# A decoder trunk on one core: the second mixer's work laid out in a table of slots, its time step on 128 columns, and a look-ahead in the residual step

## What is computed

```python
for i in range(4):
    x = x + mixer[i](rmsnorm(x, mix_norm[i]))
    x = x + conv_ffn(rmsnorm(x, ffn_norm[i]), ...)      # D_FF 2816
```

```python
z, xbc, dt_raw = split(h @ w_in)                 # 2048, 3072, 32 columns
xs, B, C = split(silu(causal_conv4(xbc)))
dt = softplus(dt_raw + dt_bias)                  # (512, 32)
cs = cumsum(dt * a) in each chunk                # a = -exp(a_log)
y = (C B^T * exp(cs_l - cs_s), causal) @ (x * dt)  +  C @ state * exp(cs)  +  x * d_skip
y = group_rmsnorm(y * silu(z)) * norm_w;  out = y @ w_out
```

## Time and profile before

| | |
|---|---|
| median of 3 runs | 2025.08 us (2021.57 to 2025.17) |
| the profiled execution | 2023.04 us, span 2021.2 us |
| busy in the span: PE, DVE, ACT, POOL | 91%, 60%, 56%, 58% |
| granted TensorE clock, mean of the execution | 0.972 of full |
| DMA, mean | 111 GB/s |

### The profile page before, as it was taken

One profiled execution on the slowest core, in us unless ns is written; L12 is line 12 of the kernel. 1 busy time (PEld: TensorE's weight loads), 2 busy tenths in 40 slices (PEclk: granted clock), 3 DMA queues, 4 the chain that ended last, 5 costly groups with the idle time before them and its releaser, 6 DMA issues.

```text
span 2021.2 us, 25413 instructions
## 1 busy us (share of the span) xinstructions
PE 1845.0 (91%) x8918; PEld 1152.6 (57%) x8918; DVE 1213.3 (60%) x1995; ACT 1132.2 (56%) x1571; POOL 1171.9 (58%) x1678
## 2 busy tenths in 40 slices
PE   6978999978888888999999778899999999879999
PEld 3544666644554554566665566466666777546665
DVE  6774777146667654577414665577526777467740
ACT  6867666436655635666545444666553444566642
POOL 4536778845334334777785201677785555367786
PEclk9999999999999989999999888999999999989999
DMA  5314444433122222444443100344443222134443
GB/s 195 104 42 146 146 146 148 155 102 105 58 68 71 66 63 84 166 147 146 145 158 105 42 1 22 116 147 149 142 157 108 84 84 84 63 115 148 148 151 127
DMA packets 64926, 225.00 MB, mean 111 GB/s; under 512 B 7328, under 2 KB 8736, under 8 KB 64544
## 3 DMA queue, kind: packets, MB, share of 16 engines
q1 hardware_dynamic: 64224, 221.69, 32.4%
q10 hardware_dynamic: 576, 1.69, 0.3%
HBM read 221.25 MB, written 2.10 MB: 110 GB/s over the span
## 4 chain that ended last, share of the span: by engine, by line
PE 66%; DVE 15%; ACT 13%; issue 5%; DMA 1%; POOL 0%; DVEq 0%; ACTq 0%; SPq 0%
PE psum L274 20%; PE psum L284 19%; PE psum L316 10%; PE psum L320 9%; PE psum L1521 3%; ACT w_big L232 2%; DVE psum L1316 1%; ACT arena L1982 1%; ACT x_big L352 1%; DVE arena L2072 1%; DVE arena L2077 1%; ACT psum L1195 1%; ACT psum L356 1%; DVE x_resid L422 1%; DVE psum L1409 1%
## 5 line engine op out<-in xcount | busy, mean ns | idle before, releaser
L248 POOL TENSOR_TENSOR w_rest<-w_panel,w_big 128x256 bf16<-128x256 f32 (+1 forms) x1674 | 1171.7, 740 | 836.5 <-ACT w_big L232 836.2
L274 PE MATMUL psum<-x_big,w_big 128*128 128x512 f32 x2248 | 667.6, 429 | 53.2 <-ACT x_big L352 37.4
L284 PE MATMUL psum<-x_rest,w_rest 128*128 128x512 bf16 x2248 | 561.2, 385 | 0.2 <-DVE x_rest L388 0.2
L232 ACT ACTIVATE w_big<-w_panel 128x1024 fp32r<-128x1024 f32 (+3 forms) x425 | 422.8, 1018 | 240.0 <-DVE x_resid L422 115.5
L274 PEld LDWEIGHTS psum<-x_big,w_big 128*128 128x128 f32 x2248 | 419.6, 190 | 186.4 <-issue 44.2
L284 PEld LDWEIGHTS psum<-x_rest,w_rest 128*128 128x128 bf16 x2248 | 190.2, 99 | 283.2 <-issue 108.0
L574 DVE SCALAR_TENSOR_TENSOR psum<-ffn_raw,params,psum 128x512 f32<-128x512 f32 x352 | 264.5, 751 | 6.2
L566 DVE TENSOR_TENSOR ffn_raw<-psum,rstd 128x512 f32<-128x512 f32 x176 | 121.7, 692 | 153.2 <-PE psum L284 132.7
L316 PE MATMUL psum<-g_big,w_big 128*128 128x512 f32 x704 | 199.3, 423 | 0.0
L528 ACT ACTIVATE psum<-ffn_raw,params 128x512 f32<-128x512 f32 x176 | 137.7, 782 | 107.3 <-DVE ffn_raw L566 106.8
L422 DVE SCALAR_TENSOR_TENSOR x_resid<-psum,x_resid 128x512 f32<-128x512 f32 x64 | 43.9, 688 | 210.6 <-PE psum L320 210.6
(11 more groups left out here) (255 smaller groups left out, 1925.1 us busy)
## 6 DMA issues: line engine op xcount, KB each, us to landing
w_panel<-in_up SPq DMA_DIRECT2D x176, 512.0 KB, 3.4
w_panel<-in_dn SPq DMA_DIRECT2D x64, 448.0 KB, 3.1
w_panel<-in_ssd_in SPq DMA_DIRECT2D x41, 512.0 KB, 3.5
w_panel<-in_dn SPq DMA_DIRECT2D x32, 512.0 KB, 3.4
w_panel<-in_hgrn_in SPq DMA_DIRECT2D x32, 512.0 KB, 3.5
w_panel<-in_lru_in SPq DMA_DIRECT2D x19, 512.0 KB, 3.4
w_panel<-in_ssd_out SPq DMA_DIRECT2D x16, 512.0 KB, 3.5
w_panel<-in_swa_in SPq DMA_DIRECT2D x12, 512.0 KB, 3.5
```

Of the source, the lines that this page charges most:

```text
L232: act.activation(k.w1[:, slot, lo:words], k.w[:, slot, lo:words], ACT.Copy, scale=(SHIFT - 1) / SHIFT).then_inc(k.s("panel_big"), 1)
L248: rest = pool.tensor_tensor(k.w2[:, slot, a], k.w[:, slot, a], k.w1[:, slot, a].bitcast(F32), ALU.subtract)
L274: pe.matmul(out, k.w1[:, slot, q * m:(q + 1) * m], k.x1[:, q, :], start=q == 0, stop=False)
L284: mm = pe.matmul(out, k.w2[:, slot, q * m:(q + 1) * m], k.x2[:, q, :], start=False, stop=q == DT - 1)
```

## The change

- **Slots.** `ssd_events()` now runs over slots n = 0 to 48. In slot n PE makes projection tile n (of 40, in three pieces of 2, 2 and 4 reduction steps), DVE scales tile n-1 (`evict`) and adds its taps, ACT adds its bias and applies silu. Group g's `turn` is in slot 10, 20, 30, 39, its states one slot later, its four pairs of heads in the four slots after that, its norm 7 slots after `turn`.
- **Gating in the next slot.** A pair's `seg`, `spread` and `out` stand in one slot; DVE's part after `out` (`post`) comes first in the next slot, then the two products of `seg`, and the three taps last. The sum of squares has an event of its own (`sum`). `finish` is cut into `normed` and `rest`, spread over two slots. The order of the tiles in a group changes (`SSD_KINDS`), and with it the order of the columns of the weight.
- **Time step on 128 columns.** The first tile holds the 32 columns four times. DVE moves chunk c (128 tokens) of copy c to partitions 32c to 32c+31, so that the chain runs on 128 partitions by 128 columns, in three pieces in slots 0 to 2; the scan needs no resets. ACT lays the three bf16 parts out again (12 copies of 32x128).
- **Selection columns.** The 128 equal columns that pick a head out of `cs3` are no longer copied out for each group (L1354, L1356): PE reads one column with a step of 0, and ACT copies out the 64-wide ones once (`pick64`).
- **Residual.** In `residual_vector`, after the output projections of mixers 1, 3 and 4, add(o) stands ahead of split(o-1) and squares(o-1). In all of them split of the last tile comes ahead of the last two sums, and ACT's last two squares and last panel come last. In the feed-forward net the norm's matmul stands after the high half of tile 1 (it stood after tile 0).

Core of the diff:

```diff
 def residual_vector(dve, k, c, job):
+    ahead = job in ("lru_out", "swa_out", "hgrn_out")
     for o in range(DT):
         add_to_residual(dve, k, job, o)
-        if c is not None:
+        if c is None:
+            continue
+        if o and ahead:
+            split_x(dve, k, c, o - 1)
+            if o < DT - 1:
+                sum_squares(dve, k, c, o - 1)
+        elif not ahead and o < DT - 1:
             split_x(dve, k, c, o)
-            sum_squares(dve, k, c, o)
+            if o < DT - 2:
+                sum_squares(dve, k, c, o)
+    if c is not None:
+        split_x(dve, k, c, DT - 1)
+        sum_squares(dve, k, c, DT - 2)
+        sum_squares(dve, k, c, DT - 1)
...
 def residual_scalar(act, k, c, job):
+    n = len(OUT_PARTS[job])
     for o in range(DT):
+        last = out_panel(job, o, n - 1)
+        if n > 1 or o == DT - 1:
+            round_ahead(act, k, job, last - 1 if n > 1 else last - 2)
+        act.wait_ge(k.s("banks_free"), k.evicted(job, o))
+        if o < DT - 2:
             round_ahead(act, k, job, last)
+        scaled_x(act, k, c, o)
+        if o < DT - 2:
+            square_x(act, k, c, o)
+    square_x(act, k, c, DT - 2)
+    square_x(act, k, c, DT - 1)
+    round_ahead(act, k, job, last)
...
 def ffn_tensor(pe, k, l):
         in_begin(pe, k, job, i)
-        in_tile(pe, k, job, i, fresh=None if i else 2 * l + 1)
-        if i == 0:
+        in_big(pe, k, job, i, fresh=None if i else 2 * l + 1)
+        if i == 1:
             norm_tensor(pe, k, 2 * l + 1)
+        pe.wait_ge(k.s("panel_split"), k.split(job, i))
+        in_rest(pe, k, job, i, fresh=None if i else 2 * l + 1)
...
+SSD_KINDS = [[6, 7, 0, 1, 2, 3, 4, 5, 8, 9]] + [[0, 1, 2, 3, 6, 4, 5, 7, 8, 9]] * (SSD_G - 1)
+SSD_LAST = 10 * SSD_G
+SSD_TURN = [10, 20, 30, 39]
...
+    head_at = {at + 2 + p: (g, p) for g, at in enumerate(SSD_TURN) for p in range(SSD_R // 2)}
+    norm_at = {at + 7: g for g, at in enumerate(SSD_TURN)}
...
+    for n in range(SSD_LAST + 9):
+        if n == SSD_LAST:
+            tiles = [[], fill(1), fill(1)]
+        elif SSD_LAST < n < SSD_LAST + 6:
+            tiles = [fill(1), [], fill(1 if n < SSD_LAST + 3 else 2)]
...
+        if n == SSD_LAST + 6:
+            ev += fill(16 - early)
...
+    def pick(self, g, r):
+        return self.pick3[0:SSD_ROWS, SSD_R * g + r:SSD_R * g + r + 1].to_broadcast([SSD_ROWS, P])
...
     def dt(g, i):
+        if i == 0:
+            dve.wait_ge(k.s("panel_used"), k.used(job, 0))
+            for c in range(NC):
+                rows, cols = slice(32 * c, 32 * c + 32), slice(c * P, (c + 1) * P)
+                dve.tensor_tensor(b.cs[rows], k.ps[rows, k.bank(job, 0), cols], k.rstd[rows, cols], ALU.mult
...
+            softplus_begin(dve, softplus, b.cs, b.size, b.dt)
+        elif i == 1:
+            softplus_ratio(dve, k, "ssd_softplus", softplus, b.size, b.e, b.q, b.e2)
+            softplus_series(dve, softplus, b.size, b.e2, (15, 13, 11, 9, 7, 5, 3))
```

More of the change, by code:

```diff
@@ L1001, in ssd_events @@
[L1001 to L1012 removed]
+    turn_at = {at: g for g, at in enumerate(SSD_TURN)}
@@ L1246, in early @@
             round_ahead(act, k, "ssd_out", len(used) - 1)
-    do = {"dt": dt, "conv": conv, "decays": decays, "turn": turn, "seg": seg, "out": out, "norm": norm,
-          "finish": finish, "early": early, "silu": silu, "spread": spread}
+    do = {"dt": dt, "cs": cs, "evict": evict, "decays": decays, "scores": scores, "seg": seg, "square": square, "root": root,
+          "normed": normed, "early": early, "silu": silu, "spread": spread, "round": round_}
     for what, g, i in ssd_events():
@@ L1426, in ssd_vector @@
+    do = {"dt": dt, "evict": evict, "taps": taps, "decays": decays, "table": table, "turn": turn, "states": states,
+          "seg": seg, "post": post, "sum": sum_, "normed": normed, "rest": rest}
     for what, g, i in ssd_events():
@@ L2302, in layout @@
         i[:, None] % SSD_DT == np.arange(SSD_DT),
[L2303 removed]
+        np.ones((P, P)),
     ], axis=1).astype(np.float32)
```

484 lines of the change are left out of this document (269 added, 215 removed).

## The result

The changed kernel takes **1924.3 us** (median of 4 runs, 1923.6 to 1925.8) against 2024.0 (4 runs, 2021.6 to 2025.2): ratio **0.951**, interval 0.949 to 0.953, 99.7 us less. The forecast was 1933 with a range of 1914 to 1964: the sign and the range hold, the size was 9 us too small. In the profiled executions the span went from 2021.2 to 1921.8, 99.4 less.

What follows compares the result with a forecast made beforehand. PE, at work nine tenths of the span, was taken as the bound. From 2023.0 us, 58.7 (second mixer) and 33.2 (look-ahead and last tile) go, leaving 1931.1; with 2.1 for the median, 1933 us, range 1914 to 1964.

Steps and rivals of the forecast that it cites:

- The large idle piece: Start of the second mixer: with the time step on 128 columns, PE's idle 15.7 us go.
- Waits inside the pairs: Second mixer's pairs of heads: PE's short waits go, with gating in the next slot; no separate size given.
- slots would be limited by DVE or ACT: Rival, second mixer: each of 16 slots with heads grows by 1.2 us; 25 us come back, 1958 us; chance 0.24.
- A new slot with a pair holds about the same: Second mixer: a new slot with a pair of heads takes about the 8.3 us measured before without a wait.
- more than forecast: Rival, second mixer: small waits under 0.3 us go too, about 13 us, giving 1920 us; chance 0.07.
- The turns: Second mixer: waits at third transposes and norms, 2.7 us; in slot 39, 3.3 us and perhaps 2 of clock.
- the 12.5 us of before: Second mixer: full-speed time lost while PE worked at the lower clock, each time after waiting about 3 us; all goes.
- The start: Second mixer: 1.5 us of waiting left before the first transposes in slot 10.
- The tail: Second mixer, before the output projection's second half: 7.8 us stay open, plus 1.7 us for the clock after it.
- The residual step: After the mixers: look-ahead and last tile give 33.2 us less, of which 10.1, 13.7 and 7.3 by look-ahead.
- The column with step 0: PE's head-selection reads: no change in time; rival that PE reads it slowly, 2045 us at 0.7 us each, chance 0.04.
- Tables: Rival, ACT in second mixer's slots: table changes cost 1.38 us of drain on top, 26 us, 1959 us; chance 0.02.

Runs made afterwards that it cites:

- Run 7: The changed kernel with the time step's chain in one row at the start instead of three pieces: 1926.6 us.
- Run 6: The changed kernel with the three taps put back ahead of gating, products and sum in DVE's row of each slot: 1938.9 us.
- Run 5: The changed kernel with the pair's row of 16 products cut in two by tile matmuls, in twelve slots with a pair and a tile: 1935.5 us.
- Run 3: The changed kernel with the first half of each norm (DVE's products, ACT's rounding copies) moved right behind the inverse root: 1918.3 us.
- run 10: The changed kernel with ACT's twelve small time-step copies in slots 8 to 10 instead of 5 to 7, the wide copy in 10: 1924.2 us.
- run 4: The changed kernel with three output-projection fills moved from slots 43 to 45 to behind the last norm's matmul: 1919.9 us.
- run 12: run 9's kernel with one more fill moved from slot 40 to behind the last norm: 1915.9 us.
- run 2: The changed kernel with the residual step of the kernel before, keeping the second mixer's new slots and time step: 1956.4 us.
- Run 11: The changed kernel with DVE's look-ahead alone taken back at the end of the first, third and fourth mixer: 1948.5 us.
- run 9: run 8's kernel with the turn's first products ahead of the norm's second half in DVE's row (slot 39: ahead of all that is left): 1911.5 us.
- run 8: The changed kernel with the moves of Run 3 and run 4, plus ACT's panel rounding ahead of the inverse root: 1914.8 us.

## Why the prediction was right, and where it was 9 us off

*The large idle piece.* Right. It went, as the time step's 15.7 us were the width of its operations. Run 7 shows that the pieces did not matter; the four banks covered the chain whole. The row is 10.0 us, a little over the 8 to 9 of the estimate.

*Waits inside the pairs.* Right, and the reason given for it too: with the taps last PE stands 0.3 us in 59. Run 6 puts a price on that one line of order, 14.6 us. The rival that slots would be limited by DVE or ACT did not come true, but the same run shows how near it was. Here luck had a part. The sum gave DVE 7.8 us in a slot of 8.3; the slot is 7.55, and DVE's 7.8 would not have gone into it. It is busy for 7.0, since operations in a row start 0.60 us apart though each lasts 0.68. And the wait of 0.85 is not most of the 44 us that the taps stood for ACT before: 24 times 0.85 is 20, and 15 of the 24 waits are longer, 1.67 to 4.69.

*"A new slot with a pair holds about the same", 8.3 us.* This is **the step that failed**. It took the length of a slot of before without a wait as PE's work, and that contains the way the work is cut. Put in rows of 16 the same products take 0.5 us less, and the rest of the slot 0.2: 7.55 us. Run 5 restores the cut of the products, and with it their 0.5. (The prediction also misread what the 8.3 us hold: two heads and one tile, 8 steps of L274, not one and a half tiles. A new slot holds one tile too, so "about the same" was right all the same.) In twelve slots 0.75 us and in the last group's four the 0.5 of the products are 11 us. PE's work at full speed without waits was 354.1 - 65.2 - 12.5 = 276.4 before and is 288.25 - 23.0 - 6.0 = 259.2 now (6.0 is the lost clock while PE worked, from windows of 4 us each, 9.2 in all less 3.1 in the gaps): 17.2 less, where the sum had none. The rival "more than forecast" had a time of 1920 and 0.07, with "small waits under 0.3 us" as its mechanism: its number was near, its mechanism was not there. In the trace of before the waits of 0.3 us and more are 65.1 of the 65.2 us of idle time. About 6 of the 17.2 are not accounted for by the slots; the groups by form put 1 us each on the carried products, the scores and the transposes, part of them run at the lower clock before. How they divide stays open.

*The turns.* Mis-sized the other way. I gave the third transposes of slots 20 and 30 0.6 us each and four norms 0.3, and wrote 2.7 for it (it is 2.4). They are 3.28 each, 6.6, and the norms wait nothing. In slot 39 I had counted DVE's nine operations and got 3.3 us; it is 5.5, and 0.6 before it, since I left out that DVE itself stands for ACT's copies. Run 3 shows that cause. The lost clock at these places, where the level of 1.2 GHz stands behind the waits of 3.28, 3.28 and 5.52 us, was 6.0 us in place of the 2 counted there. Behind the last of them:

```profile
652.79:660.50 7.71, 7.71 (x32) 5.36 (x32) 3.73 (x6) 1.40 (x3) 1.83 (x3) 0.64 0.22 68
```

Nor did all of the 12.5 us of before lie behind waits of about 3 us: from 612.66 to 616.08 the granted clock was 0.50, and no wait in the 35 us ahead of that was over 1.8.

*The start.* 2.8 us in place of 1.5. Of the two grounds named, DVE's 3.8 us a tile against PE's 3.6 and ACT's tables, the trace speaks for ACT: before its taps at 454.13 DVE itself stands 3.85 us for ACT's bias, and in ACT's row this bias stands behind two tables and four small copies. The twelve small copies take 0.31 us each (estimate 0.2, bounds 0.1 to 0.6); run 10 shows that moving them gains nothing.

*The tail.* 6.8 us where 7.8 were predicted, and 1.0 of clock behind it for 1.7. This was the "weak spot"; run 4 shows that 4.1 of the 6.8 were avoidable, and run 12 that one fill more does not get the rest.

So the second mixer comes to 295.4 - 17.2 (work) + 7.7 (idle, 23.0 for 15.3) + 2.3 (clock, 6.0 in the stretch for the 3.7 that the sum held in it) = 288.2: two errors, of 17 and 10 us, against each other. That the whole came out within 9 us is in that measure luck.

*The residual step.* Right term by term: 10.1 for 10.5, 14.3 for 14.1, 1.1 for 1.3. The first mixer's is 9.0 for 7.3, and not known better than to some 4 us: against run 2, which has the old residual step, it is 5.3 (340.0 to 334.7). Run 11 shows that DVE's queue was the cause; 24 of 31 us hang on it.

*The column with step 0.* No price, as taken: the weight load of 96x128 (L1097, now L1206) was 101 ns and is 97, and the matmul of 512 columns behind it went from 405 to 384. The Trainium skill (TensorE: Matmul & The Clock Gate, Weight-path perf modes) lists column steps from -1,023 to 1,024 for its fast load, a range that holds 0, and the trace agrees: the load of contiguous bf16 weights beside it (L1210) takes 97 ns too.

*Tables.* The load at 515.34 lasts 1.28 us and the silu behind it starts at 516.64, 1.30 after the load began. The drain of 1.38 us on top, which the Trainium skill (ScalarE: Activation LUTs, What ACT_TABLE_LOAD costs) gives, does not show here either. All 40 loads of the second mixer begin within 0.02 us of the end of the instruction before. In the 59 us around the first group's pairs there are 11 loads, by the page's figure 15.2 us of drain, and ACT is idle for 12.6.

## What to carry to other kernels

When a change regroups the matmuls of a bound engine, sum the new order from the start-to-start distances of each kind of row, not from a whole slot of before: the same 16 products took 0.5 us more in two rows than in one, and a slot "without a wait" hid it. Take an engine's share from the slot itself too: DVE was at 0.81 over 59 us and at 0.93 in the slot that mattered. Where a queue is nearly full, follow each wait two engines back: PE waited for DVE, DVE for ACT, and moving ACT's copies gave the wait to POOL. Ask of a move that gained time whether the waits went or only moved: run 9's moved. And when a table of slots drives all engines, moving an event for one of them moves what the others do for it; fills behind a norm helped until the panels' rounding, which moved along, came too late.

## What was not expected of the hardware

- 128x64 f32 products of 128 columns last 278 ns each. Within a head they start 110 ns apart, and two heads' rows back to back run in between each other: 16 in 1.52 us, where twice 8 with other matmuls between take 2.05. It shows as busy time, not as idle time, so no view of waits names it.
- DVE's operations on 128x128 take 0.3 us (seven in 2.30 us), as estimated from 0.7 at 512 columns, but a reciprocal of the same size 0.95 (3.35 on 96x512 before).
- A wait of 5.5 us cost 2.8 us more in clock (granted 0.64 over the next 7.7 us), half of the wait again. One of 2.0 us cost 1.7 in one place of run 8 (0.77 over 7.49 us) and nothing in the other.
